# Moving one channel group of a depthwise convolution from TensorE to GpSimd, and regrouping the dense products by operand

## The reference

```
h = rmsnorm(x);  z = h @ w_in           # q, k, v, g, gr (gate rank 16), ca, cb
o = gla(q, k, v, log_sigmoid(gr @ w_gate_up + b) / 16)   # 4 heads, 64 keys, 128 values
o = rmsnorm(o) * silu(g)
u = ca * sigmoid(cb)                    # 512 channels
u = causal_dwconv(u, conv_w, conv_b)    # 31 taps over the tokens, one filter per channel
u = silu(layernorm(u))                  # over the 512 channels
x = x + concat(o, u) @ w_out
layer 0: x = x + (silu(h @ wd_gate) * (h @ wd_up)) @ wd_down      # width 2816
layer 1: the same, over 8 experts, the best 2 of each token
```

## Time and profile before

| | us |
|---|---|
| median of 3 runs | 1199.09 |
| the profiled execution | 1198.86 |
| its span (first to last instruction) | 1197.0 |
| TensorE busy | 1182.3 (99%) |
| TensorE weight loads busy | 991.4 (83%) |
| VectorE busy | 989.0 (83%) |
| ScalarE busy | 783.4 (65%) |
| GpSimd busy | 93.8 (8%) |

### The profile page before, as it was taken

The page is one execution under the profiler, slowest core; times in us unless marked ns, Lnnn a source line. Parts: engine busy times, 40 slices in busy tenths (PEclk is TensorE's granted clock), DMA queues, the critical chain, the costliest instruction groups (busy, mean ns, idle before and its releaser), DMA issues.

```text
span 1197.0 us, 15673 instructions
## 1 busy us (share of the span) xinstructions
PE 1182.3 (99%) x6216; PEld 991.4 (83%) x6216; DVE 989.0 (83%) x909; ACT 783.4 (65%) x693; POOL 93.8 (8%) x160
## 2 busy tenths in 40 slices
PE   9999999999999999999999999999999999999996
PEld 8987888888898788888888888888888888888885
DVE  5988767556668889899799889879879889979987
ACT  6756544434655667677677677768668668667764
POOL 8230000000123000000000000000000000000000
PEclk9999999999999999999999999999999999999999
DMA  9972665555556279999999999999999999999980
GB/s 284 352 223 71 208 196 177 194 191 177 194 184 220 71 249 369 389 374 376 389 371 392 378 371 392 373 381 385 378 377 388 383 384 373 382 386 373 395 331 38
DMA packets 184999, 362.72 MB, mean 303 GB/s; under 512 B 10568, under 2 KB 70746, under 8 KB 184922
## 3 DMA queue, kind: packets, MB, share of 16 engines
q1 hardware_dynamic: 178170, 343.22, 80.0%
q0 software_dynamic: 6736, 18.43, 4.4%
q10 hardware_dynamic: 16, 0.00, 0.0%
HBM read 350.64 MB, written 7.86 MB: 299 GB/s over the span
## 4 chain that ended last, share of the span: by engine, by line
PE 92%; DVE 5%; ACT 2%; issue 1%; DMA 0%; ACTq 0%; DVEq 0%
PE YB L2281 18%; PE WBS L2260 13%; PE WBS L2262 13%; PE WBS L2261 13%; PE WBS L1776 6%; PE YB L1868 6%; PE WBS L1777 3%; PE YB L2272 2%; PE YB L2296 2%; PE YB L2048 1%; PE WBS L1765 1%; PE WBS L1766 1%; PE WBS L1767 1%; PE YB L1849 1%; PE WBS L1829 1%
## 5 line engine op out<-in xcount | busy, mean ns | idle before, releaser
L1019 DVE TENSOR_TENSOR w_lo<-raw,w_hi 128x2048 fp32r<-128x2048 f32 x319 | 716.1, 2285 | 82.4 <-ACT w_hi L617 82.1
L617 ACT ACTIVATE w_hi<-raw 128x2048 fp32r<-128x2048 f32 x324 | 597.6, 1915 | 6.7 <-DMA raw<-in_w_in 6.6
L2260 PE MATMUL WBS<-w_hi,t_both 128*128 128x512 f32 x704 | 278.7, 396 | 0.5 <-DVE w_lo L1019 0.5
L2262 PE MATMUL WBS<-w_hi,t_both 128*128 128x512 f32 x704 | 274.8, 390 | 0.0
L2261 PE MATMUL WBS<-w_lo,t_both 128*128 128x512 f32 x704 | 274.2, 390 | 0.0
L2260 PEld LDWEIGHTS WBS<-w_hi,t_both 128*128 128x128 f32 x704 | 132.2, 188 | 29.7 <-issue 2.8
L2262 PEld LDWEIGHTS WBS<-w_hi,t_both 128*128 128x128 f32 x704 | 132.1, 188 | 28.2
L2261 PEld LDWEIGHTS WBS<-w_lo,t_both 128*128 128x128 f32 x704 | 132.4, 188 | 26.4
L970 ACT ACTIVATE eT_hi<-YB 128x512 fp32r<-128x512 f32 (+1 forms) x48 | 27.1, 564 | 143.5 <-PE YB L2296 143.5
L1776 PE MATMUL WBS<-t_both,w_hi 128*128 128x512 f32 x304 | 107.8, 399 | 0.0
L2281 PE MATMUL YB<-w_hi,eT_hi 128*128 128x512 f32 x320 | 99.4, 392 | 0.3 <-DVE eT_lo L1689 0.3
(11 more groups left out here) (329 smaller groups left out, 1458.1 us busy)
## 6 DMA issues: line engine op xcount, KB each, us to landing
raw<-in_we_down SPq DMA_DIRECT2D x88, 1024.0 KB, 7.1
raw<-in_we_gate SPq DMA_DIRECT2D x80, 1024.0 KB, 6.9
raw<-in_we_up SPq DMA_DIRECT2D x80, 1024.0 KB, 6.9
raw<-in_w_in SPq DMA_DIRECT2D x19, 1024.0 KB, 6.1
raw<-in_wd_gate SPq DMA_DIRECT2D x11, 1024.0 KB, 5.4
raw<-in_wd_up SPq DMA_DIRECT2D x11, 1024.0 KB, 5.4
...
```

The costliest lines, as they stand in the source:

```text
L617: act.activation(w_hi[:, hi_slot(n, item), :], raw[slot][:], ACT.Copy).then_inc(hi_ready, 1)
L1019: dve.tensor_tensor(w_lo[:, slot], raw[slot][:], w_hi[:, hi_slot(n, item), :].bitcast(F32), ALU.subtract).then_inc(lo_ready, 1)
L2260: pe.matmul(bank, xs_hi[:, k0 + k, :], hi[:, k, :], start=start, stop=False)
L2262: ins = pe.matmul(bank, xs_lo[:, k0 + k, :], hi[:, k, :], start=False, stop=stop)
```

## The change

It has two parts.

- `dense_unit` issues the same 32 matmuls, but first the 16 of 512 columns and then the 16 of 256 columns.
- Group 1 of the convolution leaves TensorE (`ON_PE` is now [2, 3] in both layers). GpSimd makes it tap by tap: a `tensor_scalar` (`cu` times the tap, into one of two buffers `pool_tap` that lie in the free part of `shifted`) and a `tensor_tensor` that adds this to `acc[:, 1]`. Tap 0 is one instruction. Sixteen taps stand ahead of the DMA issues for groups 2 and 3, fifteen behind them. The 16 DMAs of group 1, 16 matmuls, one `conv_weights`, one `place` and one `add_ahead` per layer are gone. `sum_groups(0)` has a new wait for all 31 taps of GpSimd.

```diff
-    ON_PE = [[1, 2, 3], [1, 2, 3]]
+    ON_PE = [[2, 3], [2, 3]]
+        pool_tap = [shifted[:, k, 0:T] for k in range(2)]
 ...
@@ GpSimd, in each layer
-                if ON_PE[l][0] == 1:
-                    pool.wait_ge(cu_ready, 2 * l + 1)
-                    for b in range(4):
-                        for s in range(4):
-                            n = T - 3 + s
-                            pool.dma_start(shifted[32 * s:32 * (s + 1), b, APART - 1 - s:],
-                                           cu[32 * b:32 * (b + 1), 1, PAD:PAD + n]).then_inc(shifted_ready[0], 16)
+                def taps_ahead(first, last):
+                    for w in range(first, last):
+                        if w == 0:
+                            pool.tensor_scalar(acc[:, 1, :], cu[:, 1, 0:T], taps[:, l, 0, 1:2], pv[:, param(l, PV_CB, CT, 1)],
+                                               ALU.mult, ALU.add).then_inc(pool_conv, 1)
+                            continue
+                        if w > 1 or l:
+                            pool.wait_ge(pool_conv, TAPS * l + w - 1)
+                        pool.tensor_scalar(pool_tap[w % 2], cu[:, 1, w:w + T], taps[:, l, w, 1:2], None, ALU.mult).then_inc(pool_step, 1)
+                        steps[0] += 1
+                        pool.wait_ge(pool_step, steps[0])
+                        pool.wait_ge(pool_conv, TAPS * l + w)
+                        pool.tensor_tensor(acc[:, 1, :], acc[:, 1, :], pool_tap[w % 2], ALU.add).then_inc(pool_conv, 1)
+                pool.wait_ge(cu_ready, 2 * l + 1)
+                pool.wait_ge(params_ready, 1)
+                pool.wait_ge(pads_ready, 3 * l + 1)
+                taps_ahead(0, 16)
                 pool.wait_ge(cu_ready, 2 * (l + 1))
                 ...   (the 16 DMA issues of groups 2 and 3)
+                taps_ahead(16, TAPS)
 ...
@@ ScalarE: place(0), squares, roots, place(1), head_hi, place(2) become
+                    head_squares()
+                    head_roots()
+                    place(0)
+                    head_hi()
+                    place(1)
 ...
@@ VectorE, sum_groups(0)
+                        dve.wait_ge(pool_conv, TAPS * (l + 1))
@@ VectorE, layer 0 (layer 1 alike)
                     conv_weights(0, 1)
-                    conv_weights(0, 2)
                     conv(4)
-                    add_ahead(0)
                     head_sums(0)
                     head_sums(1)
                     head_gates()
-                    add_ahead(1)
+                    add_ahead(0)
 ...
@@ TensorE, dense_unit
                 for f in range(2):
                     for k in range(KD):
-                        pe.matmul(banks[:, f, :], hi[:, k, cols], t_both[:, :, k, :], start=(k == 0), stop=False)
-                        ins = pe.matmul(banks[:, f, 0:T], lo[:, k, cols], t_hi[:, k, :], start=False, stop=(k == KD - 1))
+                        pe.matmul(banks[:, f, :], hi[:, k, P * f:P * (f + 1)], t_both[:, :, k, :], start=(k == 0), stop=False)
+                for f in range(2):
+                    for k in range(KD):
+                        ins = pe.matmul(banks[:, f, 0:T], lo[:, k, P * f:P * (f + 1)], t_hi[:, k, :], start=False, stop=(k == KD - 1))
@@ TensorE, mixer: conv(2) level(8) conv(6) heads conv(11) turn_heads conv(5) become
+                conv(1)
                 level(8)
+                conv(3)
                 heads()
+                conv(9)
                 turn_heads()
+                conv(3)
```

More of the change, by code:

```diff
@@ L274, in trunk @@
             "shift_rows_ready", "shift_pads", "conv_grouped", "odd_added"))
-        shifted_ready = [sem(f"shifted_ready{g}") for g in range(2)]
+        shifted_ready, pool_conv = sem("shifted_ready"), sem("pool_conv")
         conv_step = [sem(f"conv_step{c}") for c in range(2)]
@@ L328, in param @@
             return slice(L * at0 + count * l + k, L * at0 + count * l + k + 1)
-        DVE_CONV = [[(w % 2 if ON_PE[l][0] == 1 else c, c, w) for w in range(TAPS) for c in range(ON_PE[l][0])] for l in range(L)]
+        DVE_CONV = [[(w % 2, 0, w) for w in range(TAPS)] for l in range(L)]
         PE_CONV = [[(i, c, h_, q) for i, c in enumerate(ON_PE[l]) for h_ in range(2) for q in range(QS)] for l in range(L)]
@@ L373, in conv_bank @@
         def conv_bank(l, i):
-            return WB[[3, 2, 3][i] if len(ON_PE[l]) == 3 else [3, 2][i]]
+            return WB[[3, 2][i]]
         def hi_slot(n, item=None):
@@ L546, in _ @@
                         pool.dma_start(shifted[32 * s:32 * (s + 1), 4 + b:12:4, APART - 1 - s:],
-                                       acc[32 * b:32 * (b + 1), 2:4, 0:n]).then_inc(shifted_ready[1], 16)
+                                       acc[32 * b:32 * (b + 1), 2:4, 0:n]).then_inc(shifted_ready, 16)
+                taps_ahead(16, TAPS)
                 pool.wait_ge(level_done, 9 * (l + 1))
@@ L793, in mixer @@
                     preload(ACT.Sqrt)
-                    place(0)
                     head_squares()
                     head_roots()
+                    place(0)
+                    head_hi()
                     place(1)
-                    head_hi()
-                    place(2)
                     hi(b + N_MIX)
@@ L1122, in sum_groups @@
                             dve.wait_ge(conv_step[chain], STEPS_BEFORE[chain][l + 1])
-                        if ON_PE[l][0] == 1:
-                            dve.tensor_tensor(acc[:, 0, :], acc[:, 0, :], acc_odd[:], ALU.add).then_inc(odd_added, 1)
-                            dve.wait_ge(odd_added, FIRST_BEFORE[l] + 1)
+                        dve.tensor_tensor(acc[:, 0, :], acc[:, 0, :], acc_odd[:], ALU.add).then_inc(odd_added, 1)
+                        dve.wait_ge(odd_added, l + 1)
+                        dve.wait_ge(pool_conv, TAPS * (l + 1))
                         dve.wait_ge(conv_grouped, GROUPS_BEFORE[l + 1])
@@ L1312, in mixer @@
                     sum_groups(0)
-                    add_ahead(2)
+                    add_ahead(1)
                     sum_groups(1)
@@ L1347, in mixer @@
                     conv_weights(1, 1)
-                    conv_weights(1, 2)
-                    add_ahead(0)
                     conv(3)
@@ L1974, in conv @@
                         if done[0] % (2 * QS) == 0:
-                            if c == 1:
-                                pe.wait_ge(shifted_ready[0], 16 * 16 * (FIRST_BEFORE[l] + 1))
-                            else:
-                                pe.wait_ge(shifted_ready[1], 16 * 16 * (l + 1))
+                            pe.wait_ge(shifted_ready, 16 * 16 * (l + 1))
                             pe.wait_ge(shift_w_ready, GROUPS_BEFORE[l] + i + 1)
-                            if i == 2:
-                                pe.wait_ge(conv_placed, 4 * (GROUPS_BEFORE[l] + 1))
-                                pe.wait_ge(conv_added, 4 * (GROUPS_BEFORE[l] + 1))
                         for j in range(2):
```

6 lines of the change are left out of this document (removed).

## The result

| | before | after |
|---|---|---|
| median of the runs | 1199.17 us | 1226.07 us (1223.88 to 1228.31) |
| ratio, 95% interval | | 1.0223 [1.0211, 1.0235] |
| profiled execution, its span | 1198.86, 1197.0 | 1228.31, 1226.4 |

The forecast was 1215 us with a range of 1202 to 1242. The time lies in that range, but outside the likeliest case's own range (1206 to 1224), between rival (b) (1220) and rival (c) (1233).

What follows compares the result with a forecast made beforehand. The prediction took TensorE as the bound, with VectorE also full in the token mixer. Against 1198.86 us it summed -2.2 - 4.4 + 13.0 + 7.4 + 2.4 = +16.2 to 1215 us, slower, range 1202 to 1242.

Steps and rivals of the forecast that it cites:

- likeliest case: Whole kernel: TensorE's savings are outweighed by GpSimd holding VectorE, 1215 us, own range 1206 to 1224; chance 0.46.
- rival (b): Token mixer: VectorE keeps the shared resource, so GpSimd reaches DMA issues late, near 88 us; 1220 us, chance 0.16.
- rival (c): Token mixer: GpSimd slower, 1.4 us held and 1.6 run per tap, last at `sum_groups(0)`; 1233 us, chance 0.18.
- part 1: Dense products: runs of one width take 0.347 us a pair instead of 0.354, saving 2.2 us.
- part 2: Convolution: TensorE loses group 1's matmuls, 7.3 us of work, of which 4.4 us comes back over both layers.
- part 4: Token mixer: each GpSimd tap holds VectorE 1.0 us, costing 13.0 and 7.4 us, plus 2.4 behind.
- rival (a): Token mixer: VectorE isn't held by GpSimd, so only TensorE's savings remain; 1192 us, faster, chance 0.14.
- part 3: GpSimd's own time: 31 taps take 34 us beside 8.44 us of DMA issue; undisturbed, it finishes in time.
- a tap is 1.1 us: GpSimd's convolution tap: 0.40 us one-input plus 0.62 us two-input instruction, with 0.07 for a wait.
- It just fits: End of the mixer: GpSimd ends 29 us behind `conv_input(1)`, and TensorE waits only from about 31 us.

Runs made afterwards that it cites:

- e1: The kernel before, with only its dense products regrouped into runs of one width: 1197.36 us, ratio 0.9985.
- e5: The kernel after, with GpSimd making only tap 0 of group 1 and taps 1 to 30 left out: 1192.98 us, ratio 0.9949.
- e6: The kernel after, with GpSimd's 16 taps ahead of the DMA issues kept and the 15 behind left out: 1215.23 us, ratio 1.0123.
- e9: The kernel after, with each GpSimd tensor_scalar replaced by a tensor_tensor against the repeated tap, same result: 1214.94 us, ratio 1.0133.
- e12: The kernel after, with e9's two-input taps, 20 ahead of the DMA issues and 11 behind: 1222.29 us, ratio 1.0193.
- e7: The kernel after, with tap 0 ahead of the DMA issues, taps 1 to 15 behind, the last 15 left out: 1209.06 us, ratio 1.0088.
- e3: The kernel after, with GpSimd's taps 1 to 30 replaced by memsets of about the same length that read nothing: 1203.42 us, ratio 1.0035.
- e2: The kernel after, with its dense products in turns again, so GpSimd's part only: 1227.18 us, ratio 1.0244.
- e10: The kernel after, with 10 of GpSimd's taps ahead of the DMA issues and 21 behind, same work: 1235.25 us, ratio 1.0299.

## Why the prediction was right, and where it was not

The direction was right, and the cause that the sum gave for it exists, but it is the smaller half of the loss. By the terms of the sum, in profiled runs:

| term | forecast | measured | from |
|---|---|---|---|
| part 1 | -2.2 | -1.9 | e1, third stretch (1.8 by the medians) |
| part 2 | -4.4 | -3.9 | e5, 2.1 and 1.7 |
| part 4, ahead of conv_input(1), layer 0 | +13.0 | +7.9 | 73.3 - 65.4 |
| the same, layer 1 | +7.4 | +4.1 | 251.3 - 247.2 |
| behind it, layer 0 | +1.4 | +15.7 | 63.9 - 48.2 |
| the same, layer 1 | +1.0 | +7.9 | 56.0 - 48.1 |

The measured ones sum to 29.8, against 1228.31 - 1198.86 = 29.45. VectorE's delay ahead of `conv_input(1)`, forecast at 20.4 us, is 12.0; what comes behind it, forecast at 2.4, is 23.6. Two errors of opposite sign, 8 and 21 us, made the total 13 us wrong and no more. That the time lies in the whole range is owed to rival (c), which stretched the range upward, and not to the sum.

**Part 1 and part 2** hold. e5 shows part 2 alone. Where VectorE is late at `conv_input(1)` and GpSimd doesn't decide (e6 in layer 1, e9, e12) the stretch to X is 50.1 to 50.8, about as before, so there its saving is gone again. e6 shows in layer 1 how:

```profile
386.37 1.98 PE L2049 MATMUL YB<-lnw 64*128 64x64 f32 x16 [3.32 <-DVE lnw L1190]
```

VectorE is late, TensorE idles for 3.3 us ahead of this level, and in the 4 us behind that it is granted 0.50, so the level takes 1.98 us in place of 1.06. TensorE reaches the heads 19.5 us behind `conv_input(1)` where e5 reaches them in 17.5, and the stretch is longer by the same 2.0 us (50.1 against 48.1).

**Part 4, VectorE held: right mechanism, too dear in after.** The forecast took 1.0 us a tap. A pair costs VectorE 0.71 us beside its taps. Ahead of `conv_input(1)` the delay is 7.7 us (73.3 against e7's 65.6), and 14 of the 16 taps had run by then: 0.55 each. The rows fit this: where GpSimd stands behind a whole `w_lo` it does few taps and holds VectorE little. In the two-input form (e9) all 16 are done by then and cost 12.1 us (0.76 each), and the last four of e12 0.96 each. So the two engines hold each other in both directions, e3 shows that it goes with GpSimd's reading, and rival (a) is out.

**The failed step is in part 3 and its end: "a tap is 1.1 us" and "It just fits".** The term had 29 us for GpSimd behind `conv_input(1)`, 8.4 + 15 x 1.1 + 4. It takes 45.6 in layer 0: 10.6 us until its 16 taps ahead are done at all (the prediction had them done by then; in e2's execution it is 6.8), 8.6 us of issues, and 26.4 us for 15 taps (1.76 each). In layer 1 the 16 taps are done in time and it still takes 37.0, so there the tap's price alone breaks the term. The point from which TensorE waits was well read (31 forecast, 29.5 measured); GpSimd misses it by 16 us in layer 0 and by some 8 in layer 1. The 0.40 us for a one-input instruction was extrapolated from a copy and a cast, which don't lie on one line (with the cast's 0.84 ns an element the copy of 128 would take 0.15 us, and took 0.29); it takes 0.92, and with a constant 0.85. The two-input one takes 0.72 for 0.62. The Trainium skill's page GPSIMD Engine Reference, section 3.1, had led to an estimate of 0.56 us of streaming for that; 0.72 with everything is in line with it. No row of the trace before warned of the one-input price.

**The rivals.** (c) named the mechanism, GpSimd last at `sum_groups(0)`, and its pace (1.6 us a tap for 1.71), and (b) named the other half, the late issues (88 us forecast, 83.9 measured). I had priced them as alternatives. Both are true in layer 0, and the loss isn't their sum: the late issues are part of the late end (e10). In layer 1 (b) had the issues about 10 us late, and they weren't. And (c) took 1.4 us held per tap, which no run shows. The chances should have given more to (c): its bound of the tap's own price, 2.0 us held and as much run, came from rows, and I took the low value from two operations that weren't those of the change.

**What held by its own test.** VectorE's taps above 0.48, GpSimd's instructions stretched to the length of a `w_lo`, and in layer 1 half as much ahead of `conv_input(1)` were all found. In layer 0 TensorE idles ahead of levels 3 and 5 only for 3.4 us together (2.4 of them ahead of level 3, not most ahead of level 5); the larger waits are those named for (b) and (c).
